# The fourth weight sum of each gate and up pair computed on GpSimd instead of VectorE in a two-layer decoder step

## The reference, cut to what matters

```python
def swiglu(h, wg, wu, wd):
    return (jax.nn.silu(h @ wg) * (h @ wu)) @ wd

h2 = rms_norm(x, g_ffn_l) * (1 + sc2) + sh2
if layer % 2 == 0:
    f = swiglu(h2, *ffn_w)
else:
    f = moe_swiglu(h2, *ffn_w)
x = x + gt2 * f
```

## Time and profile before

| | |
|---|---|
| Median of three runs | 1605.25 us (1603.27 to 1606.41) |
| Profiled execution: span from first to last instruction | 1600.4 us |
| The profiled execution's own time | not listed apart; the three runs above are 2.9 to 6.0 us over its span |
| PE busy | 1562.8 us (98%) |
| PEld busy | 1007.7 us (63%) |
| DVE busy | 553.8 us (35%) |
| ACT busy | 179.5 us (11%) |
| POOL busy | 69.5 us (4%), 118 instructions |
| Mean DMA rate over the span | 334 GB/s |
| Mean granted TensorE clock | 0.998 of full speed |

### The profile page before, as it was taken

One profiled execution on the slowest core, in us unless ns is written; L12 is line 12 of the kernel. 1 busy time (PEld: TensorE's weight loads), 2 busy tenths in 40 slices (PEclk: granted clock), 3 DMA queues, 4 the chain that ended last, 5 costly groups with the idle time before them and its releaser, 6 DMA issues.

```text
span 1600.4 us, 37215 instructions
## 1 busy us (share of the span) xinstructions
PE 1562.8 (98%) x16734; PEld 1007.7 (63%) x16734; DVE 553.8 (35%) x1210; ACT 179.5 (11%) x478; POOL 69.5 (4%) x118
## 2 busy tenths in 40 slices
PE   7999999999999999999999999999999999999997
PEld 3778898999997888944444444444554555555544
DVE  4468378666555784751101100110111011101133
ACT  2102303111112032131000000000000000000000
POOL 1110500000000110010000000000000000000010
PEclk9999999999999999999999999999999999999999
DMA  9999869666359746569999999999999999999995
GB/s 362 364 386 344 296 230 320 230 225 216 127 178 319 234 156 193 166 224 405 418 418 405 418 418 403 418 417 405 418 404 418 417 398 415 408 405 417 408 386 191
DMA packets 174340, 535.30 MB, mean 334 GB/s; under 512 B 12535, under 2 KB 101413, under 8 KB 161378
## 3 DMA queue, kind: packets, MB, share of 16 engines
q1 hardware_dynamic: 158706, 497.20, 81.1%
q0 software_dynamic: 8768, 28.96, 5.2%
q10 hardware_dynamic: 6704, 6.72, 1.3%
HBM read 517.47 MB, written 15.82 MB: 333 GB/s over the span
## 4 chain that ended last, share of the span: by engine, by line
PE 85%; DMA 11%; DVE 3%; issue 1%; ACT 1%; SPq 0%; DVEq 0%
PE bank L1877 31%; PE bank L1898 15%; PE bank L1191 14%; PE bank L1552 14%; DMA ring<-in_w_exp_up 8%; PE bank L1462 2%; PE bank L1732 2%; PE bank L1223 1%; DMA ring<-in_w_in 1%; DVE inv L2511 1%; PE bank L1719 1%; PE bank L1567 1%; DMA ring<-in_w_ada 1%; PE bank L1645 0%; DMA area<-in_w_exp_down 0%
## 5 line engine op out<-in xcount | busy, mean ns | idle before, releaser
L1877 PE MATMUL bank<-ring,xT 128*32 128x448 f32 x3072 | 301.2, 539 | 6.4 <-DMA ring<-in_w_exp_up 6.4
L1877 PE MATMUL bank<-ring,area 128*32 128x448 f32 x3072 | 300.8, 539 | 1.5 <-DMA ring<-in_w_exp_up 1.4
L575 DVE TENSOR_TENSOR area<-bank,area 128x448 f32<-128x448 f32 x48 | 46.0, 958 | 575.0 <-ACT area L1149 575.0
L1552 PE MATMUL bank<-hT,ring 128*128 128x264 f32 x1024 | 239.4, 389 | 4.0 <-ACT hT L892 3.7
L1898 PE MATMUL bank<-area 128*32 128x256 f32 x3840 | 225.6, 379 | 1.3 <-DMA area<-in_w_exp_down 1.3
L1552 PEld LDWEIGHTS bank<-hT,ring 128*128 128x128 f32 x1024 | 193.3, 191 | 38.9 <-issue 6.9
L1877 PEld LDWEIGHTS bank<-ring,xT 128*32 128x32 f32 x3072 | 109.8, 110 | 166.0 <-issue 157.7
L1877 PEld LDWEIGHTS bank<-ring,area 128*32 128x32 f32 x3072 | 109.5, 110 | 161.7 <-issue 154.6
L1898 PEld LDWEIGHTS bank<-area 128*32 128x32 f32 x3840 | 138.1, 110 | 99.6 <-issue 41.6
L1149 ACT ACTIVATE area<-bank 128x448 f32<-128x448 f32 x48 | 26.1, 544 | 778.8 <-PE bank L1877 778.8
L1898 PE MATMUL bank<-ring,area 128*32 128x256 f32 x1536 | 89.2, 379 | 0.6 <-DVE area L583 0.6
(11 more groups left out here) (367 smaller groups left out, 1273.0 us busy)
## 6 DMA issues: line engine op xcount, KB each, us to landing
ring<-in_w_exp_gate SPq DMA_DIRECT2D x128, 896.0 KB, 17.3
ring<-in_w_exp_up SPq DMA_DIRECT2D x128, 896.0 KB, 19.2
area<-in_w_exp_down SPq DMA_DIRECT2D x64, 1024.0 KB, 18.6
ring<-in_w_ada SPq DMA_DIRECT2D x96, 512.0 KB, 9.0
ring<-in_w_in SPq DMA_DIRECT2D x32, 1024.0 KB, 13.2
ring<-in_w_exp_down SPq DMA_DIRECT2D x32, 1024.0 KB, 19.6
area<-in_w_exp_down SPq DMA_DIRECT2D x32, 512.0 KB, 19.5
ring<-in_w_ff_gate SPq DMA_DIRECT2D x11, 1024.0 KB, 6.2
```

The source lines that it names most:

```text
L575: dve.tensor_tensor(F["act_tok"][:, t, :].rearrange("p (i n) -> p n i", i=BODY), bank[3 + t][:, 0:SLICE].rearrange("p (n i) -> p n i", i=B ...
L1552: mm = pe.matmul(bank[b][:, 0:T], w[:, c, :], hT[:, c, :], start=(c == 0), stop=(c == DC - 1))
L1877: mm = pe.matmul(bank[t + 3 * half][32 * g:32 * g + 32, 0:SLICE], tokens[:, t, 32 * r:32 * r + 32], w[half][:, SLICE * g:SLICE * (g + 1)], ...
```

## The change

GpSimd gets a loop over the pairs, behind its stores of zeros in layer 0: it waits until the first sum of the pair is done (which reads a21) and then computes a11 - a21 in place, first for gate and then for up, each with one count on a new semaphore `w_turned`. VectorE no longer makes that sum; `w_summed` counts three per pair, and all counts behind it are adapted. TensorE waits for `w_turned` ahead of the product with the fourth sum, one count per unit. The fourth sums of the down projection stay on VectorE. Beside that, three pairs of semaphores are merged: `rest_in` into `inputs_in`, `q_low_in` and `q_high_in` into `q_wide_in`, and `scaled` into `dve_step`.

```diff
@@ -304,7 +304,7 @@
-        INPUTS = 16 * 4
+        INPUTS = 16 * 7
@@ -439,7 +439,7 @@
-            return (0, 4 * OUT_UNITS + 4 * FF_PAIRS + 4 * DOWN_UNITS)[l] + out_sums.index((u, k)) + 1
+            return (0, 4 * OUT_UNITS + 3 * FF_PAIRS + 4 * DOWN_UNITS)[l] + out_sums.index((u, k)) + 1
@@ -533,7 +533,8 @@
-            base = Step(dve, s.scaled)
+            base = Step(dve, s.dve_step)
+            base.n = step.n
@@ -759,9 +760,9 @@
-            pool.dma_start(cst[:, 3 * P:lo], const_in[:, 3 * P:lo]).then_inc(s.rest_in, 16)
-            pool.dma_start(cst[:, hi:WHOLE], const_in[:, hi:WHOLE]).then_inc(s.rest_in, 16)
-            pool.dma_start(cst[0:NS, WHOLE:CW], const_in[0:NS, WHOLE:CW]).then_inc(s.rest_in, 16)
+            pool.dma_start(cst[:, 3 * P:lo], const_in[:, 3 * P:lo]).then_inc(s.inputs_in, 16)
+            pool.dma_start(cst[:, hi:WHOLE], const_in[:, hi:WHOLE]).then_inc(s.inputs_in, 16)
+            pool.dma_start(cst[0:NS, WHOLE:CW], const_in[0:NS, WHOLE:CW]).then_inc(s.inputs_in, 16)
@@ -798,8 +799,8 @@
-                        pool.dma_start(q_wide[0], q_rows[NS * l:NS * l + 4, :].partition_broadcast(P)).then_inc(s.q_low_in, 16)
-                        pool.dma_start(q_wide[1], q_rows[NS * l + 4:NS * l + NS, :].partition_broadcast(P)).then_inc(s.q_high_in, 16)
+                        pool.dma_start(q_wide[0], q_rows[NS * l:NS * l + 4, :].partition_broadcast(P)).then_inc(s.q_wide_in, 16)
+                        pool.dma_start(q_wide[1], q_rows[NS * l + 4:NS * l + NS, :].partition_broadcast(P)).then_inc(s.q_wide_in, 16)
@@ -829,6 +830,13 @@
+                    for i in range(FF_PAIRS):
+                        pool.wait_ge(s.w_summed, 4 * OUT_UNITS + 3 * i + 1)
+                        for kind in ("gate", "up"):
+                            v, arrived, count = pages_at(kind, 2 * i)
+                            pool.wait_ge(arrived, count)
+                            pool.tensor_tensor(v[:, 0:4, P:2 * P], v[:, 0:4, 0:P], v[:, 0:4, P:2 * P],
+                                               ALU.subtract).then_inc(s.w_turned, 1)
@@ -1235,13 +1243,13 @@
-                    pe.wait_ge(s.w_summed, 4 * OUT_UNITS + 4 * (u // 2) + 1)
+                    pe.wait_ge(s.w_summed, 4 * OUT_UNITS + 3 * (u // 2) + 1)
...
-                    pe.wait_ge(s.w_summed, 4 * OUT_UNITS + 4 * (u // 2) + 2)
+                    pe.wait_ge(s.w_summed, 4 * OUT_UNITS + 3 * (u // 2) + 2)
@@ -1251,12 +1259,12 @@
-                    pe.wait_ge(s.w_summed, 4 * OUT_UNITS + 4 * (u // 2) + 3)
+                    pe.wait_ge(s.w_summed, 4 * OUT_UNITS + 3 * (u // 2) + 3)
...
-                    pe.wait_ge(s.w_summed, 4 * OUT_UNITS + 4 * (u // 2) + 4)
+                    pe.wait_ge(s.w_turned, u + 1)
@@ -1297,7 +1305,7 @@
-                    w, sums_at = unit[u], 4 * FF_PAIRS + 4 * j
+                    w, sums_at = unit[u], 3 * FF_PAIRS + 4 * j
@@ -1623,7 +1631,6 @@
-                            pe.wait_ge(s.rest_in, 16 * 3)
@@ -2042,7 +2049,7 @@
-                    dve.wait_ge(s.rest_in, 16 * 3)
+                    dve.wait_ge(s.inputs_in, INPUTS)
@@ -2107,22 +2114,20 @@
                     if k == 0 and i >= 2:
                         dve.wait_ge(s.product_mm, finished[3, 2 * i - 3])
                     if k:
-                        dve.wait_ge(s.w_summed, 4 * OUT_UNITS + 4 * i + (0, 1, 2, 1)[k])
+                        dve.wait_ge(s.w_summed, 4 * OUT_UNITS + 3 * i + k)
                     for half in range(2):
                         v, arrived, count = views[half]
                         if k == 0:
                             dve.wait_ge(arrived, count)
-                        out, s2 = summed(i, min(k, 2))[:, half, :, :], summed(i, 1)[:, half, :, :]
+                        out, s2 = summed(i, k)[:, half, :, :], summed(i, 1)[:, half, :, :]
                         s1 = summed(i, 0)[:, half, :, :]
                         a11, a12, a21, a22 = v[:, 0:4, 0:P], v[:, 4:8, 0:P], v[:, 0:4, P:2 * P], v[:, 4:8, P:2 * P]
                         if k == 0:
                             r = dve.tensor_tensor(out, a21, a22, ALU.add)
                         elif k == 1:
                             r = dve.tensor_tensor(out, s1, a11, ALU.subtract)
-                        elif k == 2:
+                        else:
                             r = dve.tensor_tensor(out, a12, s2, ALU.subtract)
-                        else:
-                            r = dve.tensor_tensor(a21, a11, a21, ALU.subtract)
                         if half == 0:
                             r.then_inc(s.dve_step, 1)
                             step.n += 1
@@ -2132,7 +2137,7 @@
-                    at = 4 * FF_PAIRS + 4 * j
+                    at = 3 * FF_PAIRS + 4 * j
@@ -2202,7 +2207,6 @@
-                sum_pair(0, 3)
@@ -2235,7 +2239,8 @@
-                    more(3)
+                    if i == FF_PAIRS - 1:
+                        sum_down(0, 3)
@@ -2339,7 +2344,7 @@
-                    dve.wait_ge(s.q_low_in if b < 4 else s.q_high_in, 16 * (l + 1))
+                    dve.wait_ge(s.q_wide_in, 32 * (l + 1))
```

More of the change, by code:

```diff
@@ L285, in build @@
         bias_dram = nc.dram_tensor("bias_rows", [P, H * WL], F32, kind="Internal").ap()
-        names = """y_gated bias_in logits_kept wt_ready sq_added q_kept q_low_in q_high_in inputs_in vectors_in
-                 tokens_in rest_in tok_mm tok_out c_in pages_used input_mm c_out x_out vec_out wide_ready bias_mm
+        names = """y_gated bias_in logits_kept wt_ready sq_added q_kept q_wide_in inputs_in vectors_in
+                 tokens_in tok_mm tok_out c_in pages_used input_mm c_out x_out vec_out wide_ready bias_mm
                  bias_out bias_wrote lam_exp state_mm state_out mod_out square_out sum_mm root_out h_ready z_out
@@ L296, in build @@
                  act_e act_step y_read put_ready spread_mm spread_out turn_mm turn_out all_up_mm product_mm
-                 one_kept c11_read c12_read c22_read act_ready act_summed w_summed h_summed five_kept two_kept
-                 h_put h_in_ready y_stored y_kept y_got scaled gate_mm gate_tok_out out_stored""".split()
+                 one_kept c11_read c12_read c22_read act_ready act_summed w_summed w_turned h_summed five_kept two_kept
+                 h_put h_in_ready y_stored y_kept y_got gate_mm gate_tok_out out_stored""".split()
         s = namedtuple("Semaphores", names)(*[sem(name) for name in names])
```

## The result

The kernel after takes 1608.17 us (median of 10 runs, 1607.03 to 1611.83), beside 1605.39 us for the kernel before on the same chip (10 runs, 1603.27 to 1606.73). The ratio is 1.002, with a 95% interval of 1.0012 to 1.0029. That is 1.9 to 4.7 us more, 2.8 us (0.17%) by the medians. It lies at the edge of what I had called "no change", on the slow side, and 1.4 us above the 1606.8 us predicted.

What follows compares the result with a forecast made beforehand. TensorE was taken as the bound; removal 0, steady pairs 0, pair 0 +1.3, pair 1 +0.3, merges 0 gave +1.6 us on 1605.25, about 1606.8 us. Range: 1603.3 to 1610.2 us.

Steps and rivals of the forecast that it cites:

- no change: Whole kernel: a time within 0.2%, 3.2 us, of the kernel before; given chance 0.76.
- The bound, and the removal at 0: Dense layer's gate and up products: TensorE is the bound, so taking 14.2 us of sums off VectorE gains 0.
- t = 1.3 us: Assumed time of one GpSimd sum on 128x512 values, the middle between 0.69 and 2.00 us.
- The moved sum is in time, in steady pairs and in pair 0: GpSimd's sums are ready before TensorE's product needs them, 13.0 us available in pair 3, 7.1 in the first: cost 0.
- Steady pairs at 0: From pair 2 on, VectorE's idle time (3.06 us in pair 3) hides its delayed second sum: cost 0.
- Pair 0 at +1.3: First pair: GpSimd delays VectorE's chain before TensorE's weight loads, which has no idle time: +1.3 us, bounds 0 and 3.4.
- strict turns: GpSimd and VectorE alternating instruction by instruction at the second weight sum: +2.0 us in the first pair.
- Pair 1 at +0.3: Second pair: VectorE's two queued instructions probably keep their place, with 0.74 us of cover: +0.3 us, bounds 0 and 3.3.
- rival A: Engines alternate strictly at the second sum of pairs 0 and 1: 3.9 us slower, 1609.2 us; chance 0.20.
- The merges at 0: Merged semaphores: the first past score waits 1.5 us for the second query broadcast, covered before TensorE's use: cost 0.
- The distance of 4.9 us between span and time: Kernel before: median shown lies 4.9 us above the 1600.4 us profiled span; the forecast kept this distance.

Runs made afterwards that it cites:

- kernel with two inputs: Kernel before plus merged semaphores, VectorE keeping its fourth sums; GpSimd subtracts two 128x512 SBUF inputs twice per pair into unread scratch: 1608.07 us, beside 1604.63 before.
- writes only: Kernel before plus merged semaphores, VectorE keeping its fourth sums; GpSimd zero-fills two 128x512 stretches of unread scratch per pair: 1605.77 us, beside 1604.63 before.
- one input: Kernel before plus merged semaphores, VectorE keeping its fourth sums; GpSimd makes two 128x512 copies per pair into unread scratch: 1604.43 us, beside 1605.38 before.

## Why the prediction was right, and where it was not

**The bound, and the removal at 0: right.** TensorE bounds the stage. Taking the sums from VectorE gave nothing, in the change and, with no new wait beside it, in the kernel that waits for the third sum (ratio 0.9997). In the kernel that waits for the second sum VectorE is busy 10 us less from 270 to 399.5 us, and TensorE gains nothing there.

**t = 1.3 us: right.** A sum of GpSimd takes 1.27 us when nothing holds it (271.53) and 1.67 to 1.73 us when it has to wait for VectorE. The Trainium skill's ratio (GPSIMD Engine Reference, "Performance versus the Vector engine") gave an estimate of 1.35 us, 6% too much.

**The moved sum is in time, in steady pairs and in pair 0: right.** There is no wait of TensorE for GpSimd in any kernel, not even where GpSimd starts after the third sum.

**Steady pairs at 0: right, and with its own number.** The forecast let the second sum of pair 3 end 2.2 us later than before by turns. In after, TensorE's product is 2.66 us later than in the earlier trace rows (301.85 for 299.19). Less this shift, the second sum's end, 299.02, is 296.4, where the forecast had 296.8. Of 3.06 us of idle time 1.28 are left.

**Pair 0 at +1.3: right in size by luck.** The wait is 1.46 us. I had taken the middle between one turn and strict turns (+0.65 and +2.0); it was strict turns, each cheaper than I had priced them: 1.68 us for a turn of both engines, not 1.3 + 0.68. Over two turns that is 0.6 us, about the distance from 2.0 to 1.46.

**Pair 1 at +0.3: the step that failed.** I wrote that VectorE's two instructions are already in line "so it probably keeps its place". It doesn't: GpSimd comes in ahead of the first half (271.53, before 271.55) and again between the two, and the wait is 0.96 us. This is rival A's mechanism in full, at both of its places and in all pairs. What kept the time from its 1609.2 is the price: 1.46 + 0.96 = 2.4 us in place of 3.9. Part of it is the cheaper turns. The other part is a misread row: the cover in pair 1 is not 0.74 us but 1.12, because VectorE sat idle another 0.38 us before L2166. The sum of the forecast, 1.6, fell short by 0.8. I had given the strict turns 0.20 because the order seemed to need luck; the trace shows the alternation in every pair. The 1608.17 us measured are 1.4 from the forecast and 1.0 from rival A's number, so that the forecast's "no change" held, by a hair, is luck too.

**The merges at 0: right by the median**, with the broadcast late as forecast (111.54 us for the start of the past scores, 111.1 predicted). But the nearest use by TensorE was misread: in the one profiled execution that used up the cover, the waits stand at 145.60 and 150.40 us, at the products behind L2395, and not near 169.

**The distance of 4.9 us between span and time: wrong as a reading.** It is 1.7 us; the rest was that the profiled execution of before had been a short one. It did no harm, since the difference was put on the median.

## What to carry to other kernels

Before a VectorE instruction is moved to GpSimd, look for what VectorE does at that time: here GpSimd's instructions that read SBUF held back the two-input SBUF sums of VectorE beside them, and 14.2 us of work removed became 19.6 us of stretching. It cost only where VectorE had no idle time before the bound engine needed its result, here in the first two rounds of the pipeline, so cost the first rounds one by one. The remedy is to choose what GpSimd waits for so that it meets slack, PSUM reads or nothing, and not to cut its work into smaller pieces; and where VectorE isn't the bound, as here, the whole move gains nothing even then.

## What the runs showed of the hardware that was not expected

**The engines alternate, instruction by instruction.** Two VectorE instructions issued back to back do not keep GpSimd out: with two of each, the order in time is GpSimd, VectorE, GpSimd, VectorE, in 2.95 + 0.54 = 3.5 us, where the four have 2 x 1.27 + 2 x 0.68 = 3.9 us one by one. VectorE ends 0.54 us after GpSimd, in place of its 0.68.

**VectorE's PSUM reads pass.** L2171, L2176 and L2181 read one input from PSUM and one from SBUF. In the kernel after they stand at 0.28 to 0.30 us also beside a GpSimd sum (at 295.75 us for instance, with GpSimd at work from 295.52 on).

**Stretched time counts as busy.** The profile books the time in which VectorE is held back as busy time, so the page of after shows an engine that does less work and is busier (559.7 us for 553.8). The mean of one instruction (683 to 1568 ns) tells it; the share of the span does not.

**GpSimd has a new entry ahead of the first sum.** The line of GpSimd's sum in the trace of after (count, min/median/max ns, start of the first and the last):

```profile
L838 POOL TENSOR_TENSOR ring<-ring x22: 1272/1688/1727, 260.5 to 393.3; 128x512 f32<-128x512 f32 x22
L838 POOLq MODIFY_POOL_CONFIG  x2: 1468/1468/1468, 193.9 to 193.9; - x2
```

The second row stands at 193.9 us, beside the last store of zeros (issued at 193.27) and 66 us before the first sum starts, so its 1.47 us cost nothing here. The kernel with two inputs has the same entry under GpSimd's line (1.46 us, at 194.1), those with writes only and with one input have none. What a first sum wanted at once would pay for it was not tried.
